# Weight splits in 1024-column pieces, made up to five ahead, on one 1 MB ring for all stages

## The reference

```
x = first_block(x, ...)    # 2 layers: mLSTM, then GLA mixer; after each, x = LN(ALPHA*x + y);
                           # then MoE: 16 experts, each takes its 32 best tokens,
                           # swiglu of 1024 hidden columns, x = LN(ALPHA*x + moe)
x = second_block(x, ...)   # layer 0: compressed/selected/window attention + memory attention
                           # layer 1: retention + memory attention
return third_block(x, ...) # x += 0.5*swiglu; mixer; x += 0.5*swiglu   (twice)
                           # mixer 0: pooling and convolution, mixer 1: attention on chosen keys
```

```
def swiglu(h, w_gate, w_up, w_down):
    return (jax.nn.silu(h @ w_gate) * (h @ w_up)) @ w_down      # 1024 -> 2816 -> 1024
```

## Time and profile before

| | |
|---|---|
| median of three runs | 2970.84 us (2970.17 to 2972.79) |
| span of the profiled execution | 2972.5 us, the same as the slowest of the three runs to 0.3 us |
| PE busy | 2382.3 us, 80% |
| DVE, ACT busy | 1300.9 us (44%), 980.6 us (33%) |
| the two MoE layers | 155 to 652 us and 814 to 1315 us; DMA share about 1, 419 to 422 GB/s |
| mixers of the first two blocks | 0 to 155, 652 to 814, 1315 to 1877 us |
| the four FFNs and the two mixers of the third block | 1877 to 2972 us |

### The profile page before, as it was taken

The page is one execution under the profiler, slowest core; times in us unless marked ns, Lnnn a source line. Parts: engine busy times, 40 slices in busy tenths (PEclk is TensorE's granted clock), DMA queues, the critical chain, the costliest instruction groups (busy, mean ns, idle before and its releaser), DMA issues. The chain is left out here.

```text
span 2972.5 us, 33569 instructions
## 1 busy us (share of the span) xinstructions
PE 2382.3 (80%) x13393; PEld 1740.5 (59%) x13393; DVE 1300.9 (44%) x2056; ACT 980.6 (33%) x1638; POOL 22.4 (1%) x18
## 2 busy tenths in 40 slices
PE   8887555657876656649888988899879999987998
PEld 7752111126642213118767777787768888875887
DVE  5630000035622000024664554675667567465674
ACT  4420000015510000013444433544555454433543
POOL 0010000000010000000000000000000000000000
PEclk9977778778978778777988999999999999987999
DMA  6469999974469999984423443454236545561453
GB/s 229 158 270 421 421 422 422 421 297 159 192 278 419 420 420 419 422 312 116 117 83 132 144 159 127 132 198 156 90 121 210 193 142 198 159 195 33 159 198 121
DMA packets 277072, 689.98 MB, mean 232 GB/s; under 512 B 22193, under 2 KB 181889, under 8 KB 227664
## 3 DMA queue, kind: packets, MB, share of 16 engines
q1 hardware_dynamic: 276944, 688.20, 61.6%
HBM read 687.09 MB, written 5.28 MB: 233 GB/s over the span
## 5 line engine op out<-in xcount | busy, mean ns | idle before, releaser
L339 DVE TENSOR_TENSOR weight_quarters<-weight_ring,weight_quarters 128x1024 fp32r<-128x1024 f32 (+4 forms) x512 | 605.6, 1190 | 578.9 <-ACT weight_quarters L328 566.0
L328 ACT CAST weight_quarters<-weight_ring 128x1024 fp32r<-128x1024 f32 (+4 forms) x512 | 520.6, 1022 | 699.2 <-PE accumulators L3283 242.1
L3281 PE MATMUL accumulators<-xT_halves,weight_quarters 128*128 128x512 f32 x1408 | 497.7, 398 | 9.3 <-DVEq L3337 9.3
L1671 PE MATMUL accumulators<-weight_ring,arena 128*32 128x512 f32 x2048 | 333.6, 812 | 202.5 <-DMA weight_ring<-in_moe_w_up 101.7
L3283 PE MATMUL accumulators<-xT_halves,weight_quarters 128*128 128x256 f32 x1408 | 396.9, 282 | 0.0
L966 PE MATMUL accumulators<-weight_quarters,arena_halves 128*128 128x512 f32 x1552 | 362.2, 394 | 8.8 <-PEq L220 8.8
L1671 PEld LDWEIGHTS accumulators<-weight_ring,arena 128*32 128x32 f32 x2048 | 87.8, 143 | 436.9 <-issue 436.2
L966 PEld LDWEIGHTS accumulators<-weight_quarters,arena_halves 128*128 128x128 f32 x1552 | 295.4, 191 | 72.0 <-issue 9.9
L3281 PEld LDWEIGHTS accumulators<-xT_halves,weight_quarters 128*128 128x128 f32 x1408 | 266.2, 189 | 72.6 <-issue 10.0
L2423 PE MATMUL accumulators<-xT_halves,weight_quarters 128*128 128x256 f32 x2040 | 276.9, 298 | 15.1 <-DVE weight_quarters L339 10.9
L2423 PEld LDWEIGHTS accumulators<-xT_halves,weight_quarters 128*128 128x128 f32 x2040 | 267.2, 205 | 22.0 <-issue 9.9
(11 more groups left out here) (429 smaller groups left out, 2096.7 us busy)
## 6 DMA issues: line engine op xcount, KB each, us to landing
weight_ring<-in_moe_w_gate SPq DMA_DIRECT2D x64, 2048.0 KB, 19.7
weight_ring<-in_moe_w_up SPq DMA_DIRECT2D x64, 2048.0 KB, 21.1
weight_ring<-in_moe_w_down SPq DMA_DIRECT2D x64, 2048.0 KB, 21.4
weight_ring<-in_ffn_w_gate SPq DMA_DIRECT2D x44, 1024.0 KB, 5.3
weight_ring<-in_ffn_w_up SPq DMA_DIRECT2D x44, 1024.0 KB, 7.8
weight_ring<-in_ffn_w_down SPq DMA_DIRECT2D x20, 2048.0 KB, 7.9
weight_ring<-in_l_w_in SPq DMA_DIRECT2D x13, 2048.0 KB, 7.6
weight_ring<-in_mlstm_w_in SPq DMA_DIRECT2D x6, 2048.0 KB, 7.8
```

The costliest lines, as they stand in the source:

```text
L328: act.copy(high, raw).then_inc(self.m.high_ready, 1)
L339: dve.tensor_tensor(low, raw, high, ALU.subtract).then_inc(self.m.low_ready, 1)
L1671: last = pe.matmul(acc[e * CAP:(e + 1) * CAP, half * BANK:(half + 1) * BANK], tokens, w4[e][:, c * D + half * BANK:c * D + (half + 1) * BANK],
L3281: pe.matmul(out.rearrange("p (x t) -> p x t", x=2), gs.quarter(k, 0)[:, c, :], m.xT_r[:, :, c, :], start=(c == 0), stop=False)
```

## The change

**The ring.** Twelve slots of 1 MB in one sequence over all stages (`add_unit`). A split unit goes to one of 9 slots, a MoE unit to any of 12. The low part is written over the raw weights in the slot itself, and slots 9 to 11 hold six buffers for high parts. ACT makes a piece when its buffer is free, up to five pieces ahead of PE within a stage (LEAD) and four or two for the next stage. `quarter_used`, `unit_used` become one count, `weights_used`. SP issues all loads by one list, units of the next stage as soon as their slot is free.

**FFN.** Three 256-column matmuls for each 128 output rows and each c, into one accumulator (`three`); ACT applies silu to it directly, no cross halves; written out instead of looped.

**Others.** MoE gathers in plain fp32 (16 matmuls for the first quad, then 128x384 at once); the norm rows, and the gate weights of GLA, are loaded within the stream of expert weights and not behind it; the memory input of the next layer is loaded at the stage's start; the first pieces of the next stream are made behind the tail of MoE and not ahead of it; after the first MoE layer the tail makes high and low of x in 128x128 tiles straight from the accumulators. mLSTM's scores are plain fp32 on q and k that aren't split, and DVE's constants come later than the gate weights. The column order that the attention layer wants is made by its DMAs (64-column pieces) and no longer by ACT and DVE (L326, L337). The two stages of the pooling projection become one.

```diff
+    def add_unit(self, stream, u, parts, sizes):
+        slots = range(RING) if sizes else range(SLOTS)
+        slot = min(slots, key=lambda i: (self.free_at[i], i))
+        after = self.free_at[slot]
+        self.loads[slot] += 16 * len(parts)
+        pieces = []
+        at = 0
+        for size in sizes:
+            q = min(range(HIGHS), key=lambda i: (self.high_free[i], i))
+            home = RING + q // 2
+            piece = Piece(len(self.pieces), stream, u, at, size, q, max(self.high_free[q], self.free_at[home]))
+            self.use_count += 1
+            self.high_free[q] = self.use_count
+            self.pieces.append(piece)
+            pieces.append(piece)
+            at += size
+        if not sizes:
+            self.use_count += 1
+            if slot >= RING:
+                for q in (2 * (slot - RING), 2 * (slot - RING) + 1):
+                    after = max(after, self.high_free[q])
+                    self.high_free[q] = self.use_count
+        self.free_at[slot] = self.use_count
+        self.units.append((stream, u, after))
+        return slot, self.loads[slot], self.use_count, pieces
...
+    def highs(self, act, end):
+        while self.highs_made < min(end, len(self.pieces)):
+            p = self.pieces[self.highs_made]
+            if p.start == 0:
+                p.stream.wait_loaded(act, p.unit)
+            if p.after > 0:
+                act.wait_ge(self.used, p.after)
+            act.copy(p.high(), p.raw()).then_inc(self.high_ready, 1)
+            self.highs_made += 1
+    def lows(self, dve, end):
+        while self.lows_made < min(end, len(self.pieces)):
+            p = self.pieces[self.lows_made]
+            dve.wait_ge(self.high_ready, p.n + 1)
+            dve.tensor_tensor(p.low(), p.raw(), p.high().bitcast(F32), ALU.subtract).then_inc(self.low_ready, 1)
+            self.lows_made += 1
...
+    def low(self):
+        return self.stream.m.ring_r[:, self.stream.slots[self.unit], self.start:self.start + self.size]
...
-        if not (isinstance(q, int) and q < 4):
-            act.wait_ge(self.m.quarter_used, q - 3)
...
-        if k == 3 or last:
-            dve.wait_ge(self.m.low_ready, q + 1)
-            dve.sem_inc(self.m.unit_used, 1)
...
+    def fill(self, sp, u):
+        self.m.load_units(sp, self.end[min(u, self.n) - 1] if u > 0 else self.begin)
...
+def expert_stream(m, wg, wu, wd):
+    ws = [w.rearrange("(q e) (p a c) n -> q a e p (c n)", e=EQ, p=P, c=2) for w in (wg, wu, wd)]
+    return Stream(m, [[(lambda slot: slot, w[q, a, e])] for q in range(QUADS) for w in ws for a in range(DC // 2) for e in range(EQ)])
...
+def three(pe, out, left, right, start, stop, **kw):
+    for i, (a, b) in enumerate(PASSES):
+        last = pe.matmul(out, left[a], right[b], start=(start and i == 0), stop=(stop and i == 2), **kw)
...
+        def high(t, c):
+            act.wait_ge(s["turned"], (DC * t + c) // 2 + 1)
+            act.activation(m.xT_r[:, c, 0, t * P:(t + 1) * P], self.turn(t, c), ACT.Identity, scale=self.g[:, c:c + 1],
+                           bias=self.b[:, c:c + 1]).then_inc(s["scalar_moved"], 1)
...
-                dve.tensor_tensor(self.parts[:, 1, t], m.x[:, t, :], self.parts[:, 0, t].bitcast(F32),
-                                  ALU.subtract).then_inc(s["parts_low"], 1)
...
-            stream.high_ahead(act)
             tail.scalar(act, s)
+            m.highs(act, stream_after(m, stream).piece(2))
...
-                    out = m.ps[:, 4 * j + k, :]
...
+                    out = m.ps[:, u % 2 * 2 + part, :]
+                    pieces = gs.pieces[2 * u + part]
...
+                        w = [x.rearrange("p (c n) -> p c n", c=4)[:, c % 4] for x in (p.high(), p.low())]
+                        for f in range(2):
+                            last = three(pe, out[:, f * T:(f + 1) * T], [x[:, f * P:(f + 1) * P] for x in w], [m.xT_r[:, c, k, :] for k in range(2)],
+                                         f == 0 and c == 0, c == DC - 1, skip_group_check=True)
+                        if c % 4 == 3:
+                            last.then_inc(m.used, 1)
...
-                        pe.matmul(out.rearrange("p (x t) -> p x t", x=2), gs.quarter(k, 0)[:, c, :], m.xT_r[:, :, c, :],
-                                  start=(c == 0), stop=False)
-                        last = pe.matmul(out[:, T:2 * T], gs.quarter(k, 1)[:, c, :], m.xT_r[:, 0, c, :], start=False,
-                                         stop=(c == DC - 1))
-                    last.then_inc(m.quarter_used, 1)
...
-                act.copy(cross[:, k], m.ps[:, 4 * j + 2 * k:4 * j + 2 * k + 2, T:2 * T]).then_inc(
-                    s["up_cross"] if k else s["gate_cross"], 1)
...
+                m.highs(act, gs.piece(4 * u + 2 + LEAD))
+                gs.wait_used(act, 2 * u)
+                if u >= 2:
+                    act.wait_ge(s["hidden"], u - 1)
+                act.activation(gate[:, u % 2, :], m.ps[:, u % 2 * 2, :], ACT.Silu).then_inc(s["silu_out"], 1)
...
-                dve.tensor_tensor(gate[:, j], m.ps[:, 4 * j:4 * j + 2, 0:T], cross[:, 0], ALU.add).then_inc(s["gate_freed"], 1)
...
-                dve.tensor_tensor(up, m.ps[:, 4 * j + 2:4 * j + 4, 0:T], cross[:, 1], ALU.add).then_inc(s["up_freed"], 1)
...
+                m.lows(dve, gs.piece(4 * u + 4 + LEAD) - 1)
+                gs.wait_used(dve, 2 * u + 1)
                 dve.wait_ge(s["silu_out"], u + 1)
-                link = chain(dve, s["hidden_steps"], u * 3)
-                link(dve.tensor_tensor(prod, gate[:, j], up, ALU.mult))
...
```

More of the change, by code:

```diff
@@ L720, in scalar @@
             root(1, 1)
+        if self.gain is not None:
             for t in range(TT):
-                for c in range(DC):
+                for c in range(ahead if t == 0 else 0, DC):
                     high(t, c)
@@ new lines, in normed, with product, begin @@
+        if self.into == "router":
+            for t in range(TT):
+                for c in (0, 1, 4, 5):
+                    dve.wait_ge(s["turned"], (DC * t + c) // 2 + 1)
+                    dve.tensor_scalar(m.xT[:, c, t * P:(t + 1) * P], self.turn(t, c), self.g[:, c:c + 1], self.b[:, c:c + 1],
+                                      ALU.mult, ALU.add).then_inc(s["vector_moved"], 1)
+def out_matmuls(m, stream, pe, s, chunks, lhs, bank, hidden=None, before=None):
+    def product(i, t, h, first, last):
+        p = stream.pieces[i // 2][i % 2]
+        right = [x[:, h * BANK:(h + 1) * BANK] for x in (p.high(), p.low())]
+        return three(pe, m.ps[:, bank + 2 * t + h, :], lhs(i, t), right, first, last)
+    def begin(i):
@@ L972, in out_matmuls @@
         if hidden and i % 2 == 0:
             hidden(pe, i // 2)
+        stream.pieces[i // 2][i % 2].wait(pe)
+    for i in range(chunks - 2):
+        begin(i)
         for t in (1, 0) if before and i == 0 else (0, 1):
@@ L3358, in after @@
-            def after(k, g, j):
-                if k == 1:
-                    gate_sum(g, j)
-                if k == 3:
-                    hidden(g, j)
-            def unit(g, j):
-                for k in range(first(g, j), 4):
-                    gs.low_part(dve, g, j, k)
-                    if not (isinstance(g, int) and g == 0 and j == 0):
-                        after(k, *back(g, j))
-            gs.each(dve, unit, peel=True)
-            for i in range(FFC):
-                ds.low_part(dve, i // 8, i // 4 % 2, i % 4, last=(i == FFC - 1))
-                if i < 4:
-                    after(i, *end)
@@ new lines, in pool_conv, with _ @@
+    with m.stage("pool_conv_in", *proj.names) as (block, s):
+        @block.sync
+        def _(sp):
+            in_stream.fill(sp, in_stream.n)
+        @block.tensor
+        def _(pe):
+            for u in range(3):
+                for k in range(4):
+                    proj.quarter(pe, s, u, k)
+        @block.scalar
+        def _(act):
+            for u in range(3):
+                for k in range(4):
+                    proj.highs(act, u, k)
+                    if u > 0 and k == 0:
+                        proj.leave_scalar(act, s, u - 1)
+            proj.leave_scalar(act, s, 2)
+        @block.vector
+        def _(dve):
+            for u in range(3):
+                for k in range(4):
+                    proj.lows(dve, u, k)
@@ L3892, in _ @@
                     act.copy(place(0, t, c), pair(t, c)).then_inc(s["high_moved"], 1)
-            for k in range(first.ready_made):
-                first.high_part(act, 0, 0, k, first.first_width)
+            m.highs(act, 1)
         @block.vector
```

1337 lines of the change are left out of this document (509 added, 828 removed).

## The result

| | before | after |
|---|---|---|
| median | 2970.5 us (2966.4 to 2972.8, 4 runs) | 2945.2 us (2944.5 to 2946.5, 4 runs) |
| span of the profiled execution | 2972.5 | 2944.7 |

The ratio is 0.9916, with a 95% interval of 0.9901 to 0.9930: 25 us faster. The forecast was 2954 (2925 to 2988), faster with 0.62. The direction was right, and so was the main part, the chains of the mixers. Their size was put too low, and one wait that the change adds, of SP, was not seen.

A forecast was written before the change was run, and what follows sets the result against it. DMA bytes were taken to bound the MoE layers, matmul pitch the FFNs, and PE's waits on DVE to mark the mixers. Terms +14 −5 −3 −22 +4.6 −6 +0 = −17; 2972.5 − 17 − 1.7 = 2954 us, range 2925 to 2988.

The forecast's parts named there:

- FFN, +14: FFN gate/up halves: 4224 matmuls of 256 columns at 0.120 us, paced by weight loads, make 511.5 against 497.5 us, +14.
- Rival A: FFNs: each matmul with its load costs more than 120 ns; at 0.130 the FFNs cost +56, total 2996 us; chance 0.10.
- Start, −5: Kernel start: PE's first gate product no longer waits for DVE's constants and can start at about 11, −5 us.
- Scores and gathers, −3: mLSTM's scores −1 us; MoE gathers in plain fp32 −2, as 16 matmuls save operand switches, 1 us once a layer.
- Chains of the mixers, −22: Five mixers: ACT's wait for the quarter PE is using falls out of the chain, −22 us, bounds −49 and 0.
- gaps shorter by a third at the successors of L2728, L1879 and L1216: Mixers: expected sign of the forecast, PE's gaps at the lines replacing these three shorter by a third.
- The sign for a wrong forecast: Mixers: the forecast is wrong if PE's waits on DVE sum to what they were; FFN windows staying at 122 also counted.
- Into GLA, +2: First MoE layer's tail into GLA: 32 DVE operations cost about +5, shorter waits for gate weights and low parts offset, net +2.
- Norm rows, +2.6: MoE layers: 1 MB of norm rows inside the bounding stream costs 2.5 us in the first layer, 0 in the second.
- End of the second MoE layer, −6: Second MoE layer's tail can begin 9.2 us earlier, before the low parts, which gives −6; bounds −9.2 and 0.
- Pooling, 0: Pooling: one stage end less, some −3, but the rest of its loads later by as much; 0, bounds −4 and +4.
- rival B: MoE layers: 1 MB loads don't fill the queues; a gap of 0.4 us per added DMA gives 3031 us; chance 0.05.

## Why the prediction was right, point by point

*FFN, +14.* Right: the gate/up windows rose by 12.9, the stages by 11.1. 4224 matmuls at 0.120, and the loads as the bound, are what the windows after show, PEld busy 128.30 of 128.30 us. Rival A didn't come, although DVE writes the low parts into the ring that PE reads. By the Trainium skill (TensorE: Matmul & The Clock Gate, Back-to-back issue gap), load and matmul together set the spacing; the trace agrees. By the 262 cycles (109 ns) that it gives for the matmul alone, an estimate, the 4224 matmuls would have taken 460 us, 50 less than the 510.4 measured.

*Start, −5.* PE's first gate product came 6.1 earlier, and the wait ahead of it shrank by 5.3. Right.

*Scores and gathers, −3.* The scores were not measured by themselves. Wrong for the gathers. After, 16 fp32 matmuls stand as 32 records:

```profile
159.81 7.91 PE L1363 MATMUL accumulators<-arena,x 128*128 128x128 f32 x32 [0.99 <-DVEq L1543]
```

7.91 against the 7.94 of the earlier trace rows, and the first expert matmul came 0.8 to 1.0 us later in its stage than before. PEld is busy for 7.72 of the 7.91 us, as it was for 7.75 of 7.94 before, and the records follow each other every 0.24 us in both, although the mean granted clock over the row was 0.64 after and 0.50 before. By this the 32 weight loads set the time here, and they have not become fewer. What an fp32 matmul costs by itself this row doesn't say.

*Chains of the mixers, −22.* The step held in kind and was under-sized: the term that failed in size is "a little under half". The stages lost 33.2, and the runs with four buffers and with six ahead put the wait at 33 to 36 us in the changed kernel, not 22. By stage, forecast and measured: mLSTM −3 and −2.7, GLA −3 and −10.4, attention −6 and −4.9, retention −4 and −10.1, selected attention −6 and −5.1. So the miss lies in GLA and retention, where PE's idle time fell by 5.9 and 7.1.

The other thing missing is that I priced waits only by their length. PE's busy time in the five mixers fell by 16.4 us, as much as its idle time without the start (16.8). How much of that is clock is not separated: in mLSTM with six ahead most of the loss is, but between before and after GLA's mean clock even fell (0.90 to 0.88) while its busy time shrank.

The places that I named are not where it happened. The sign was gaps shorter by a third at the successors of L2728, L1879 and L1216. It failed at all three. L1216's two waits fell from 5.9 to 4.8 us in all, and the others, which the earlier trace rows has with 31.0 and 8.1, stand after the change as

```profile
PE accumulators L2479 <- DVEq L2459: 29.8, 17, 5.0
...
PE accumulators L1670 <- DVE arena L1849: 10.9, 2, 9.2
```

What went are waits of GLA and retention that no row of the prediction shows, such as L1891's and L2618's above. In the attention layer PE's idle time rose by 1.2, so its −4.9 is not a shorter wait. The sign for a wrong forecast, that the waits of PE on DVE in the mixers sum to what they were, didn't come either: they sum to 89.1 instead of 113.6 us. Of this difference 10.9 are two waits, at the start of GLA and of retention, that now stand under another name, and 13.6 are real. At the place of the earlier trace rows the wait shrank by 0.57 us and did not fall out of the chain, as I had told it; ACT and DVE still wait there, a little less. There are also two such waits in mLSTM, 5.9 us together, and not three of 3.3, so that the bound of −49 was some 4 too low.

*Into GLA, +2.* DVE's 32 operations took 10.5 us as estimated (16 pairs at 0.65), and L2423's stall of 5.47 is gone: PE's wait of 11.58 stands in place of 5.12 and 5.47, +1.0. Right.

*Norm rows, +2.6.* The MoE stage grew by 3.7, of which 0.8 is the gather. The rest can't be given to the rows: the first expert layer took 464.3 to 467.5 us from run to run with the rows where the change has them.

*End of the second MoE layer, −6.* Measured −1.7 in the norm stage. The tail did begin 9.2 earlier against the scatter product, and the low parts gave back what was said. What failed is the sentence "what is late next: the highs": it was SP. I had named the 64-column pieces and their landing, but not counted their issues. One issue of the earlier trace rows takes 0.42, and 37 at that price are 15.5 us, which would still have fitted ahead of DVE's end; in this place they took 0.39 to 0.98 each, 0.64 on average, 24 us in all, longer than the tail. The run that released SP got 4.1 back, and −1.7 and −4.1 make −5.8: without SP's issues the term was right.

*Pooling, 0.* −2.0, within its bounds.

*1 MB loads (rival B).* It didn't come. The MoE windows after have 411 GB/s and a DMA share of 1.00 over the whole stage, next stage's weights included, and 421 GB/s from 200 to 600 us, where the earlier trace rows has 420 before. The Trainium skill (DMA: Bandwidth & Descriptors, Measured) gives 341 GB/s for a transfer of 1 MB issued by GpSimd. Here SP issues the loads and several are under way, and the trace doesn't show that loss.

*The sum.* It came within 9 us partly by luck. The chains were put 11 too low, and the waits of SP (4) stood against that; the terms in between missed by 1 to 4 each, to both sides.

## What to carry to other kernels

When an engine prepares data for another in a ring and has other work in its list, let it wait only for a buffer that was given back at least a step ago. One buffer more than pieces ahead was worth 35 us here, three pieces ahead or five made no difference that could be told. Count the DMA issues of a stage like the work of any engine, since the stage ends with the last of them. And when three narrow matmuls replace a wide and a narrow one, look at the weight loads, which set the pitch here (0.120 us a load, PEld busy without a gap).

## What was unexpected of the hardware

At one place of mLSTM a wait of PE of 3.26 us was followed by 11.2 us at a mean clock of 0.55 in two profiles and 0.85 in one, with matmuls at half the full rate where it was low; a wait of 2.69 us by 1.00 in five and 0.85 in two. So the same instructions behind the same wait ran at different clocks from one execution to another, and in these ten profiles half a microsecond of waiting shifted the odds. And stages with the same instructions and nearly the same idle time differed by up to 4 us between executions (the attention stage 220.9 at a clock of 0.90 and 29.2 idle in the changed kernel, 224.7 at 0.88 and 28.7 idle with the norm rows late), which is as much as most single edits here were worth.
